# The 64x64 block products of a chunked recurrence, moved from two quarters of the TensorE array to four

## The reference

```python
def rwkv7_scan(r, w, k, v, a, b):
    def step(S, inp):
        r_t, w_t, k_t, v_t, a_t, b_t = inp
        sa = jnp.einsum('bhvk,bhk->bhv', S, a_t)
        S = S * w_t[:, :, None, :] + sa[..., None] * b_t[:, :, None, :] + v_t[..., None] * k_t[:, :, None, :]
        y = jnp.einsum('bhvk,bhk->bhv', S, r_t)
        return S, y
    ...
    _, y = lax.scan(step, s0, xs)
```

## Time and profile before

| | us |
|---|---|
| median of 3 runs | 1630.02 (1629.66 to 1630.18) |
| the profiled execution | 1628.56 |
| its span in the trace | 1626.8 |
| PE busy in the span | 1578.1 (97%) |
| DVE busy | 1085.5 (67%) |
| ACT busy | 419.6 (26%) |
| recurrence, 338.5 to 653.0 us of the span | 314.5 |

### The profile page before, as it was taken

The page is one execution under the profiler, slowest core; times in us unless marked ns, Lnnn a source line. Parts: engine busy times, 40 slices in busy tenths (PEclk is TensorE's granted clock), DMA queues, the critical chain, the costliest instruction groups (busy, mean ns, idle before and its releaser), DMA issues.

```text
span 1626.8 us, 23931 instructions
## 1 busy us (share of the span) xinstructions
PE 1578.1 (97%) x9234; PEld 1136.0 (70%) x9234; DVE 1085.5 (67%) x2134; ACT 419.6 (26%) x812; POOL 133.8 (8%) x125
## 2 busy tenths in 40 slices
PE   7999999999999999999999989999999999999997
PEld 6885544467777777768644566468877888888885
DVE  5966758954545454568769896465768887886453
ACT  3345374520111110310245665301211000000000
POOL 0020020030000000000028500000000000000000
PEclk9999999999999999999999999999999999999998
DMA  7222111101111111232212222122021222223221
GB/s 265 71 81 69 55 57 58 53 27 58 37 51 41 41 41 40 97 117 91 91 52 68 88 78 92 63 67 78 27 91 65 102 80 78 104 79 96 86 91 65
DMA packets 48721, 121.63 MB, mean 75 GB/s; under 512 B 5408, under 2 KB 19488, under 8 KB 48352
## 3 DMA queue, kind: packets, MB, share of 16 engines
q1 hardware_dynamic: 47520, 116.41, 21.0%
q10 hardware_dynamic: 864, 2.37, 0.4%
q0 software_dynamic: 224, 1.31, 0.2%
HBM read 117.98 MB, written 2.10 MB: 74 GB/s over the span
## 4 chain that ended last, share of the span: by engine, by line
PE 81%; DVE 14%; ACT 1%; issue 1%; DMA 1%; SPq 0%; POOL 0%; DVEq 0%; ACTq 0%; POOLq 0%
PE bank L617 15%; PE bank L757 6%; PE vpair L1329 4%; PE opair L1329 4%; PE abank L1329 3%; PE bank L1329 3%; PE vpair L647 3%; PE opair L647 3%; DVE arena L1890 3%; DVE arena L1899 2%; PE abank L1079 2%; PE vpair L1079 2%; PE opair L1358 2%; PE vpair L1358 2%; PE vpair L691 2%; PE abank L647 2%
## 5 line engine op out<-in xcount | busy, mean ns | idle before, releaser
L617 PE MATMUL bank<-h,ring 128*128 128x512 f32 x560 | 254.2, 596 | 0.8 <-ACTq L1478 0.8
L617 PEld LDWEIGHTS bank<-h,ring 128*128 128x128 f32 x560 | 102.8, 190 | 115.7 <-issue 111.4
L1890 DVE TENSOR_TENSOR arena<-ring 128x512 f32<-128x512 f32 (+2 forms) x148 | 90.3, 610 | 73.9 <-DMA ring<-weights 47.6
L1890 DVE TENSOR_TENSOR arena<-arena,vpair 128x256 f32<-128x256 f32 x87 | 36.6, 421 | 133.7 <-PE vpair L1079 79.2
L617 PE MATMUL bank<-arena,ring 128*128 128x512 f32 (+1 forms) x320 | 121.0, 518 | 1.4 <-ACT arena L1482 1.4
L1899 DVE SCALAR_TENSOR_TENSOR arena<-arena,cols 128x512 f32<-128x512 f32 (+1 forms) x129 | 94.8, 735 | 4.6
L617 PEld LDWEIGHTS bank<-arena,ring 128*128 128x128 f32 x320 | 57.3, 190 | 41.4 <-issue 35.7
L2862 POOL TENSOR_TENSOR arena<-arena 128x512 f32<-128x512 f32 x47 | 61.6, 1311 | 10.4 <-ACT arena L1756 6.9
L1890 DVE TENSOR_TENSOR arena<-arena 128x256 f32<-128x256 f32 (+1 forms) x114 | 57.6, 505 | 7.1 <-PE bank L977 3.3
L1689 ACT ACTIVATE arena<-abank 128x256 f32<-128x256 f32 x40 | 15.4, 384 | 152.9 <-PE abank L1079 152.9
L2841 POOL TENSOR_TENSOR arena<-arena,cst 128x256 f32<-128x256 f32 x40 | 31.4, 785 | 247.8 <-issue 123.2
(11 more groups left out here) (376 smaller groups left out, 3202.8 us busy)
## 6 DMA issues: line engine op xcount, KB each, us to landing
ring<-weights SPq DMA_DIRECT2D x169, 512.0 KB, 3.6
ring<-weights SPq DMA_DIRECT2D x36, 256.0 KB, 3.3
ring<-weights SPq DMA_DIRECT2D x68, 128.0 KB, 2.3
x<-xt SPq DMA_DIRECT2D x8, 512.0 KB, 7.2
ring<-weights SPq DMA_DIRECT2D x40, 64.0 KB, 2.0
out<-h SPq DMA_DIRECT2D x8, 256.0 KB, 2.0
cst<-cst_in ACTq DMA_DIRECT2D x1, 1056.0 KB, 9.9
arena<-mem2t POOLq DMA_DIRECT2D x1, 1024.0 KB, 5.1
```

The costliest lines, as they stand in the source:

```text
L617: last = mm(o[:, 0:n], weight(), src, start=c == 0, stop=c == len(srcs) - 1)
L1890: do(V.tensor_tensor(out, a, b, op), sig)
```

## The change

Products whose eight blocks used the two diagonal quarters now use all four: for heads 2 and 3 of a pass the chunks lie crossed, either in the operands or in the output (`quad_products`). This holds for `ML`·`XX`, `AK`·`vT`, `XT`·`YT` and `XT`·`aT`; `YT`·`XT` stays on the diagonal. Heads 0 and 1 write one bank of a pair, heads 2 and 3 the other, so the a-ring becomes one tensor of two banks, and the products take pairs. `YT`·`XT` moves to the o-ring, and the gram of k and r moves from round 1 (o-ring) to round 5 (v-ring). A third, crossed gram makes `XT` for heads 2 and 3 (`crossed_gram`), and ACT writes half of `aT` crossed, in three copies instead of one. The state matrices take a pair each, chunk 0 in one bank and chunk 1 in the other; the waits of `other_rows` are gone, and DVE writes `MT` in one instruction.

```diff
-                        o = take_bank("a")
-                        a_done.inc(chunk_products(o, ML[:, n_ml % 5], XX))
+                        o = take_pair("a")
+                        for last in quad_products(o, ML[:, n_ml % 5], XX, False, True):
+                            a_done.inc(last)
...
                         if l < 5:
-                            o = take_bank("v")
-                            v_done.inc(chunk_products(o, XT, YT))
-                        o = take_bank("v")
-                        v_done.inc(chunk_products(o, YT, XT))
-                        if l == 1:
-                            o = take_pair("o")
+                            o = take_pair("v")
+                            for last in quad_products(o, XT, YT, True, False):
+                                v_done.inc(last)
+                        o = take_bank("o")
+                        o_done.inc(chunk_products(o, YT, XT))
+                        if l == 5:
+                            o = take_pair("v")
                             for last in gram(o, 0, k, r):
-                                o_done.inc(last)
+                                v_done.inc(last)
...
+                    def crossed_gram(o, lhs, rhs):
+                        done = []
+                        for j, (hd, i, p0) in enumerate(heads[2:]):
+                            for c in range(2):
+                                cols_ = tok(2 * t + c, C)
+                                last = mm(o[64 - 64 * c:128 - 64 * c, j, 4 * C:5 * C], lhs[p0:p0 + 64, i, cols_], rhs[p0:p0 + 64, i, cols_],
+                                          start=True, stop=True)
+                            done.append(last)
+                        return done
+
+                    def quad_products(o, lhs, rhs, crossed_in, crossed_out, n=C):
+                        last = [None, None]
+                        for a in range(2):
+                            for c in range(2):
+                                for g in range(2):
+                                    k0, m0 = 64 * (c ^ g if crossed_in else c), 64 * (c ^ g if crossed_out else c)
+                                    last[g] = mm(o[m0:m0 + 64, g, a * n:(a + 1) * n], lhs[k0:k0 + 64, 2 * g + a, :],
+                                                 rhs[k0:k0 + 64, 2 * g + a, :], start=True, stop=True)
+                        return last
...
-                    o = take_bank("v")
-                    for c in range(2):
-                        cr = slice(64 * c, 64 * c + 64)
-                        if c:
-                            other_rows(last)
-                        for j, (hd, i, p0) in enumerate(heads):
-                            q0 = (c * 2 + j // 2) * HD
-                            last = mm(o[p0:p0 + 64, q0:q0 + HD], WU[cr, j, 0:HD], bT[cr, tok(hd, HD)], start=True, stop=True)
-                    v_done.inc(last)
...
+                    o = take_pair("o")
+                    last = [None, None]
+                    for a in range(2):
+                        for c in range(2):
+                            cr = slice(64 * c, 64 * c + 64)
+                            for j in (2 * a, 2 * a + 1):
+                                hd, _, p0 = heads[j]
+                                last[c] = mm(o[p0:p0 + 64, c, tok(a, HD)], WU[cr, j, 0:HD], bT[cr, tok(hd, HD)], start=True, stop=True)
...
+                    o = take_pair("v")
...
+            def crossed(dst, src):
+                do(fn(dst[:, :, 0], src[:, :, 0], ACT.Copy))
+                do(fn(dst[0:64, :, 1], src[64:128, :, 1], ACT.Copy))
+                do(fn(dst[64:128, :, 1], src[0:64, :, 1], ACT.Copy), tm_ready)
...
-                    tt(tmp[:, 1, 0:4 * HD].rearrange("p (q d) -> p q d", q=4), o[:, 0:4 * HD].rearrange("p (q d) -> p q d", q=4), eye64, ADD, v_read)
-                    mt = MT[:, :, 2 * hb * HD:2 * (hb + 1) * HD]
-                    copy(mt, tmp[:, 1, 0:4 * HD].rearrange("p (c d) -> p c d", c=2))
+                    tt(MT[:, :, heads_of_hb].rearrange("p c (j d) -> p c j d", j=2),
+                       o[:, :, 0:2 * HD].rearrange("p c (j d) -> p c j d", j=2), eye64, ADD, o_read)
```

More of the change, by code:

```diff
@@ L244, in build @@
         vpair = ctx.enter_context(nc.psum_tensor("vpair", [P, 2, T], f32))
-        apair = [ctx.enter_context(nc.psum_tensor(f"abank{i}", [P, T], f32)) for i in range(2)]
+        apair = ctx.enter_context(nc.psum_tensor("apair", [P, 2, T], f32))
         opair = ctx.enter_context(nc.psum_tensor("opair", [P, 2, T], f32))
-        bank += [vpair[:, 0, :], vpair[:, 1, :], *apair, opair[:, 0, :], opair[:, 1, :]]
+        bank += [vpair[:, 0, :], vpair[:, 1, :], apair[:, 0, :], apair[:, 1, :], opair[:, 0, :], opair[:, 1, :]]
         def col(name, i=0, n=1, of=cols):
@@ L856, in dense_tokens @@
                     pass
-            def other_rows(last):
-                pe_rows.inc(last)
-                pe.wait_ge(pe_rows.sem, pe_rows.n)
             rings = {"v": (2, v_done, v_read), "a": (4, a_done, a_read), "o": (6, o_done, o_read)}
@@ L1087, in _ @@
                     chunk_gram(o, 0, bb, kk)
-                    for last in chunk_gram(o, 1, kk, bb):
+                    chunk_gram(o, 1, kk, bb)
+                    for last in crossed_gram(o, bb, kk):
                         v_done.inc(last)
@@ L1109, in _ @@
                             pe.wait_ge(tm_ready.sem, 4 * (t + 1))
-                            o = take_bank("a")
+                            o = take_pair("a")
                             vh = vT[:, 4 * hb * HD:4 * (hb + 1) * HD].rearrange("p (h d) -> p h d", h=4)
-                            a_done.inc(chunk_products(o, AK, vh))
+                            for last in quad_products(o, AK, vh, False, True):
+                                a_done.inc(last)
                         pe.wait_ge(y_ready.sem, n_ml)
@@ L1126, in _ @@
                     pe.wait_ge(av_ready.sem, it + 1)
-                    o = take_bank("a")
-                    a_done.inc(chunk_products(o, XT, aT[:, 4 * hb:4 * hb + 4, :], P))
+                    o = take_pair("a")
+                    for last in quad_products(o, XT, aT[:, 4 * hb:4 * hb + 4, :], True, False, P):
+                        a_done.inc(last)
                     fill(work)
@@ new lines, in _ @@
+                    for ins in last:
+                        o_done.inc(ins)
+                    o = take_pair("v")
+                    for a in range(2):
+                        for c in range(2):
+                            cr = slice(64 * c, 64 * c + 64)
+                            for j in (2 * a, 2 * a + 1):
+                                hd, _, p0 = heads[j]
+                                mm(o[p0:p0 + 64, c, tok(a, HD)], bT[cr, tok(hd, HD)], WU[cr, j, HD:P], start=True, stop=False)
+                                last[c] = mm(o[p0:p0 + 64, c, tok(a, HD)], kT[cr, tok(hd, HD)], vT[cr, tok(hd, HD)], start=False, stop=True)
@@ L1161, in _ @@
+                    for ins in last:
+                        v_done.inc(ins)
                     fill(work, 1 if hb and 0 < t < NT - 1 else 2)
@@ L1559, in attention, with a_read_inc, a_pair @@
                 read_through(reading, stage_, 4 * len(stage_))
-            def a_read_inc():
-                act.sem_inc(a_read.sem, 1)
-                a_read.n += 1
+            def a_read_inc(n=1):
+                act.sem_inc(a_read.sem, n)
+                a_read.n += n
+            def a_pair():
+                st["a"] += 2
+                act.wait_ge(a_done.sem, st["a"])
+                return apair
+            def crossed(dst, src):
+                do(fn(dst[:, :, 0], src[:, :, 0], ACT.Copy))
+                do(fn(dst[0:64, :, 1], src[64:128, :, 1], ACT.Copy))
+                do(fn(dst[64:128, :, 1], src[0:64, :, 1], ACT.Copy), tm_ready)
             act.dma_start(cols[:, :], cols_d).then_inc(cols_in.sem, 16)
@@ L2362, in o_pair, with o_single @@
                 return opair
+            def o_single():
+                st["o"] += 1
+                dve.wait_ge(o_done.sem, st["o"])
+                return bank[6 + (st["o"] - 1) % 2]
             incl = mask4(con("inclT"))
```

67 lines of the change are left out of this document (38 added, 29 removed).

## The result

The changed kernel takes 1615.12 us (median of 4 runs, 1613.56 to 1615.73); the kernel before takes 1630.10 beside it (1629.66 to 1630.98). The ratio is 0.9906, with the interval 0.9889 to 0.9923: faster by 15.0 us, where 20.1 were predicted. The profiled execution took 1615.73 us, the longest of the four, with a span of 1613.9.

What follows compares the result with a forecast made beforehand. PE was taken as the bound, busy 97% of the span. Eight passes at -3.05 us give -24.4; +0.6 for the crossed gram and +3.7 for copies make -20.1: 1609.9 us, forecast 1605.5 to 1614.5, wider range 1603 to 1619.

Steps and rivals of the forecast that it cites:

- The price of a product: Products on four quarters: 14 ns a matmul against 26 on the diagonal, so 16 records take 0.21 us less.
- round ends: From `XT`·`YT` to the next `ML`·`XX`: about 1.11 us, from 1.32 in rounds 2 to 4 and 1.67 in round 1.
- the rival of gains lost behind waits: Ends of rounds keep their 1.32 us and `XT`·`aT` gains nothing: 10 us gained, 1620 us; chance 0.13.
- `XT`·`aT`: Product of 128 columns, 1.03 us before: on four quarters -0.41 us a pass, between no gain and -0.43.
- State matrices: `MT` and `NN`: 2.11 us becomes 1.28, -0.83 a pass, with `NN` still waiting for DVE's copy of the outputs.
- The moved gram and the crossed gram: Gram of k and r covers nothing in round 5: +0.64 us a pass; crossed gram 0.11 us, +0.6 in all.
- The crossed copies: ACT's three copies for one delay the first `ML`·`XX` in each tile's first pass: +3.7 us in all (+1.4 to +4.5).
- the step that carries the whole difference to the end: What follows the recurrence is not edited and starts when the last state is carried, so the whole difference reaches the end.

Runs made afterwards that it cites:

- two-quarter kernel: The changed kernel with all crossings undone (products, gram, copies), so products use the two diagonal quarters; order, pairs and counts stay: 1634.24 us.
- split kernel: The changed kernel with two of the four transposes ahead of the first opening fill and two between the fills: 1605.97 us.
- extra matmuls: The changed kernel with five never-read matmuls per tile behind the last three groups of transposes, where PE waits for ACT: 1613.45 us.
- early gram: The changed kernel with the gram of k and r among the opening grams instead of behind round 5: 1614.11 us.
- half fills: The changed kernel with the fill of rounds 2 to 5 cut in two, one part ahead of `ML`·`XX`, one behind: 1611.95 us.
- one copy: The changed kernel with PE crossing `kk` by identity matmuls and ACT making one copy of 512 columns instead of three of 256: 1609.97 us.

## Why the prediction was right and where it was not

- *The price of a product.* Right: 0.39 us measured for 0.40, and the round ends of 1.03 and 1.16 us for 1.11. That the wait at the round's end stays was right too; the rival of gains lost behind waits is out. The two-quarter kernel shows that this term carries all of the gain. The rule of the Trainium skill that the prediction weighed ("TensorE: Matmul & The Clock Gate", Part 3 on row and column tiling) would have made `ML`·`XX`, whose neighbours share their rows, no faster; the trace disagrees here as in the gram: 0.39 us against 0.63 on two quarters.
- *`XT`·`aT`.* Predicted -0.41; from 1.03 to 0.60 us (403.08 to 403.68), -0.43.
- *State matrices.* Right in seven passes (1.35 us up to the fill for the 1.28). In the second DVE's copy starts 0.35 late, and `NN` with it; in the sixth it is DVE's add of round 2 that starts 0.35 late: 0.7 us in all. A transfer of the instruction queue lies at that place in the second pass (0.02 MB at about 406.7); that it is the cause was not tried.
- *The moved gram and the crossed gram.* Second passes gained 2.56 and 2.91 twice each, where -3.05 + 0.11 = -2.94 was predicted: apart from DVE's two late starts, as worked out.
- *The crossed copies: the step that failed.* The copies themselves are right: 0.38 us each on 64 or 128 partitions, and in the tiles that kept their clock a first pass gained 1.84 where -1.95 was predicted. The split kernel gets 1.2 us back in these. The prediction took the stand for one wait at the first `ML`·`XX`; it is three, as the last two groups of transposes wait for ACT too. That changes its length little. What the term lacked is the clock. The prediction priced a stand of PE as its own length and let everything behind it run at the full clock. In the first and third pass the clock fell behind the stand, and the pass lost about 1.64 us more: -0.80 and -0.21 measured for -2.5 and -1.95.

In the profiled recurrence that makes 3.3 us of clock, 0.7 of late starts and some 0.5 of small differences: 4.5 of the distance between -20.1 and -15.6. Behind the recurrence the profiled execution loses 1.65 more at 996.9 and about 1.1 at 1601, so that it ends 12.8 us ahead of the profiled one before; the medians differ by 15.0. So the step that carries the whole difference to the end did not hold in this execution either.

The time of 1615.12 us lies outside the forecast's own 1605.5 to 1614.5 us. It lies inside the wider range because that made room for a gain left behind waits, which is not what happened. That the range held is in part luck.

What stays open is where the clock falls. In the recurrence the same stand is followed by it in the first and third pass and not in the fifth and seventh. At 996.9 it follows one wait for ACT, and the kernel before has the same wait in the same stage, without a fall behind it (first the changed kernel, then the one before):

```profile
996.50 1.72 PE L931 MATMUL opair<-arena 128*64 128x128 f32 x16 [1.94 <-ACT arena L1580]
```

```profile
1012.06 1.09 PE L937 MATMUL opair<-arena 128*64 128x128 f32 x16 [1.94 <-ACT arena L1558]
```

The extra matmuls, the early gram and the half fills have a fall there as well (at 992 to 997 us), the one copy has one at 925, and the profiles of the others have none between the recurrence and the end. In its last 6 to 14 us every profile has the half level, the one before too. Nor does the kernel before always keep its clock: of its 15 executions beside the experiments three ran at a mean of 0.994, the others at 0.997 or 0.998. So the length of a wait does not tell alone whether the clock falls: the place of the fall differs from edit to edit, and from execution to execution.

The waits and the transposes between them are not fully separated. The kernel before has the same transposes with shorter waits (0.70 us in its third pass against 1.95) and kept its clock there. But each edit of the changed kernel that kept it in the recurrence also put other matmuls beside the transposes, or in place of some.

## What to carry to other kernels

When an edit shortens the bottleneck engine's work and lengthens a stand of it, price the stand twice, once as time and once as the clock behind it, and look at the granted clock right behind every place where the engine waits, again and again, between short groups. Transposes whose copies another engine makes were better issued ahead of long work than behind it: that reordering alone took 7.5 us from the recurrence here, of which some 3.3 were clock. To learn what a layout gives, run the same instruction order without it; the two-quarter kernel told the gain from the cost of its preparations.

## What the runs showed that was not expected

In the recurrence the half level followed PE's short waits for another engine (0.38, 0.68 and 0.89 us between groups), none as long as the split kernel's single wait of 1.52 us, behind which the clock stayed. The Trainium skill, "TensorE: Matmul & The Clock Gate", Part 1 on the failure mode of cycling through PSUM, describes this: short idle times between groups of matmuls can make the clock swing between its two levels. The trace of the recurrence agrees, and prices one such swing at about 1.64 us, 3.3 to 3.4 us long; in the kernel with extra matmuls in these gaps it is gone from there. Behind the recurrence, though, the half level followed a single wait of 1.94 us in some profiles and not in others. It varies by execution: the same kernel with the early gram took 1607.96 us at a mean clock of 0.997 and 1615.94 at 0.992.
